# Weight slabs in a four-block transformer kernel: the low half written in place over the raw slab, slots refilled once their matmuls are done, high halves made three slabs ahead

## What is computed

```
def swiglu(h, w_gate, w_up, w_down):
    return (jax.nn.silu(h @ w_gate) * (h @ w_up)) @ w_down

def conformer_conv(h, w_pw1, b_pw1, w_dw, b_dw, ln_g, ln_b, w_pw2, b_pw2):
    u = h @ w_pw1 + b_pw1
    a, gate = jnp.split(u, 2, axis=-1)
    u = a * jax.nn.sigmoid(gate)
    u = lax.conv_general_dilated(
        u, w_dw[:, None, :].astype(u.dtype), window_strides=(1,),
        padding=((CONV_WIDTH - 1, 0),),
        dimension_numbers=("NWC", "WIO", "NWC"),
        feature_group_count=D_MODEL) + b_dw
    u = jax.nn.silu(layer_norm(u, ln_g, ln_b))
    return u @ w_pw2 + b_pw2
```

## Time and profile before

| | us |
|---|---|
| runs of the kernel before | 3374.32, 3394.07, 3396.99 |
| their median | 3394.07 |
| span of the profiled execution | 3392.2 |
| PE busy | 3157.2 |
| PE weight load busy | 2432.9 |
| DVE busy | 1679.6 |
| ACT busy | 1250.1 |
| POOL busy | 1270.3 |

### The profile page before, as it was taken

How to read it: one execution, slowest core, us unless ns; L and a number is a source line. 1 busy time by engine, 2 the same in 40 slices (tenths; PEclk the granted TensorE clock), 3 DMA queues, 4 the chain that set the end, 5 groups by cost and what they waited for, 6 DMA issues and landing times.

```text
span 3392.2 us, 41307 instructions
## 1 busy us (share of the span) xinstructions
PE 3157.2 (93%) x13970; PEld 2432.9 (72%) x13970; DVE 1679.6 (50%) x2266; ACT 1250.1 (37%) x1983; POOL 1270.3 (37%) x496
## 2 busy tenths in 40 slices
PE   7999999989898899999986899999989789899998
PEld 5656788866675578888754777888867468778886
DVE  6455555356517745443587635222353784352224
ACT  4344444223334424432322433443222443344422
POOL 3201444433431144434576423443433125144443
PEclk9998999999998999999998899999999899999999
DMA  3201222222220022223212311222322013122222
GB/s 138 90 11 35 89 93 93 83 84 74 90 72 1 9 91 93 89 87 90 75 49 69 104 64 66 95 93 82 93 87 78 32 45 111 44 93 92 93 80 75
DMA packets 73430, 257.30 MB, mean 76 GB/s; under 512 B 8544, under 2 KB 8808, under 8 KB 72944
## 3 DMA queue, kind: packets, MB, share of 16 engines
q1 hardware_dynamic: 68400, 244.87, 22.0%
q10 hardware_dynamic: 4928, 11.10, 0.9%
HBM read 253.82 MB, written 2.12 MB: 75 GB/s over the span
## 4 chain that ended last, share of the span: by engine, by line
PE 58%; issue 22%; DVE 9%; POOL 8%; ACT 2%; ACTq 1%; DVEq 0%; DMA 0%; POOLq 0%
PE bank L564 17%; PE bank L565 17%; PE bank L566 17%; POOL w_lo L499 7%; PE bank L613 1%; PE bank L640 1%; PE bank L774 1%; DVE xl L958 1%; DVE acc L965 1%; DVE a_stat L1021 1%; POOL m_lo L515 1%; ACT sq L1569 1%; PE bank L886 1%; DVE xt L991 1%; DVE a_prob_t L1046 0%
## 5 line engine op out<-in xcount | busy, mean ns | idle before, releaser
L499 POOL TENSOR_TENSOR w_lo<-w_raw,w_hi 128x1024 fp32r<-128x1024 f32 (+1 forms) x475 | 1212.0, 2560 | 1962.3 <-ACT w_hi L1578 1962.2
L564 PE MATMUL bank<-xh,w_hi 128*128 128x512 f32 x2328 | 949.3, 408 | 85.8 <-DVE xl L958 38.2
L565 PE MATMUL bank<-xl,w_hi 128*128 128x512 f32 x2328 | 930.4, 400 | 0.0
L566 PE MATMUL bank<-xh,w_lo 128*128 128x512 f32 x2328 | 929.9, 399 | 0.0
L1578 ACT ACTIVATE w_hi<-w_raw 128x1024 fp32r<-128x1024 f32 x475 | 493.8, 1054 | 1036.3 <-DVE xt L991 540.1
L564 PEld LDWEIGHTS bank<-xh,w_hi 128*128 128x128 f32 x2328 | 443.8, 191 | 218.8 <-issue 44.3
L565 PEld LDWEIGHTS bank<-xl,w_hi 128*128 128x128 f32 x2328 | 444.1, 191 | 111.9 <-issue 7.3
L566 PEld LDWEIGHTS bank<-xh,w_lo 128*128 128x128 f32 x2328 | 443.1, 190 | 108.6
L965 DVE TENSOR_TENSOR acc<-acc,sq 128x512 f32<-128x512 f32 x88 | 185.6, 2109 | 206.1 <-ACT sq L1569 206.1
L566 PE MATMUL bank<-hh,w_lo 128*128 128x512 f32 x704 | 279.1, 396 | 0.0
L564 PE MATMUL bank<-hh,w_hi 128*128 128x512 f32 x704 | 279.1, 396 | 0.0
(11 more groups left out here) (264 smaller groups left out, 4049.0 us busy)
## 6 DMA issues: line engine op xcount, KB each, us to landing
w_raw<-w_ffn_in SPq DMA_DIRECT2D x88, 512.0 KB, 3.4
w_raw<-w_glu_in SPq DMA_DIRECT2D x88, 512.0 KB, 3.4
w_raw<-w_ssm_in SPq DMA_DIRECT2D x41, 512.0 KB, 3.4
w_raw<-w_ffn_out SPq DMA_DIRECT2D x32, 512.0 KB, 3.6
w_raw<-w_mem_kv SPq DMA_DIRECT2D x32, 512.0 KB, 3.5
w_raw<-w_glu_out SPq DMA_DIRECT2D x32, 512.0 KB, 3.6
w_raw<-w_pw SPq DMA_DIRECT2D x24, 512.0 KB, 3.4
w_raw<-w_attn_in SPq DMA_DIRECT2D x18, 512.0 KB, 3.4
```

The lines of the kernel that those rows point to most:

```text
L499: pool.tensor_tensor(w_lo[:, slot, n], w_raw[:, slot, n], w_hi[:, slot, n].bitcast(F32), ALU.subtract).then_inc(w_split, 1)
L564: pe.matmul(b, wh, hi[:, k, 0:n], start=(k == 0), stop=False)
L565: pe.matmul(b, wh, lo[:, k, 0:n], start=False, stop=False)
L566: mm = pe.matmul(b, wl, hi[:, k, 0:n], start=False, stop=last)
```

## The change

`w_lo` now lies at the address of `w_raw`, so that POOL writes the low half over the raw slab it reads (`LEAD` = 3 is new). SP may therefore load slab s only once TensorE has used slab s-4, and waits for `w_used` in place of `w_split`. ACT makes halves three slabs ahead, not four: `next_half` in step c makes slab c+3 (with one slab per chunk). The wait for `w_used` of slab s-4 in `half` stays. In `residual`, `taps`, `gate`, `attn` and `ffn` the call of `next_half` moves ahead of the wait for the bank, and the second call in `ffn` ahead of the wait for `f_prod`. POOL's inserted work (`m_lo`, and the weights of the SSM stage) comes before the fourth slab of its stream, not the fifth. Weights with 22 blocks are padded with zeros to 24 on the host, so that every slab is loaded and split at full width; TensorE still multiplies 22. The 16 KB per partition that `w_lo` had are left free.

```diff
SLAB = 8
+LEAD = 3
...
         xt = sb("xt", [P, KD, S])
+        raw_at = cursor[0]
         w_raw = sb("w_raw", [P, SLOTS, SLAB * P])
         w_hi = sb("w_hi", [P, SLOTS, SLAB * P], F32R)
-        w_lo = sb("w_lo", [P, SLOTS, SLAB * P], F32R)
+        w_lo = nc.alloc_sbuf_tensor_at("w_lo", [P, SLOTS, SLAB * P], F32R, offset=raw_at)
...
                 def turn(i, chunks):
                     for j in range(chunks):
-                        k = 0
-                        for t, nb in enumerate(st.slabs):
+                        for t in range(st.per):
                             o = j * st.per + t
                             slot = (st.slab0 + o) % SLOTS
 
-                            sp.wait_ge(w_split, st.slab0 + o + 1 + i * 4 * st.per)
-                            src = w[ds(4 * i + j, 1), :, k * P:(k + nb) * P] if not isinstance(i, int) \
-                                else w[4 * i + j:4 * i + j + 1, :, k * P:(k + nb) * P]
-                            sp.dma_start(w_raw[:, slot, 0:nb * P], src.rearrange("a p n -> (a p) n")) \
+                            sp.wait_ge(w_used, st.slab0 + o + 1 + i * 4 * st.per)
+                            ks = slice(t * SLAB * P, (t + 1) * SLAB * P)
+                            src = w[ds(4 * i + j, 1), :, ks] if not isinstance(i, int) \
+                                else w[4 * i + j:4 * i + j + 1, :, ks]
+                            sp.dma_start(w_raw[:, slot, :], src.rearrange("a p n -> (a p) n")) \
                                 .then_inc(w_landed[slot], 16)
-                            k += nb
...
-                            if between is not None and o == SLOTS:
+                            if between is not None and o == LEAD:
                                 between()
                             s = st.slab0 + o
                             slot = s % SLOTS
-                            n = slice(0, nb * P)
-
                             pool.wait_ge(w_half, s + 1 + i * 4 * st.per)
-                            pool.tensor_tensor(w_lo[:, slot, n], w_raw[:, slot, n], w_hi[:, slot, n].bitcast(F32),
+                            pool.tensor_tensor(w_lo[:, slot, :], w_raw[:, slot, :], w_hi[:, slot, :].bitcast(F32),
                                                ALU.subtract).then_inc(w_split, 1)
...
             def next_half(st, j, i):
 
                 for t in range(st.per):
-                    o = st.slab0 + j * st.per + t + SLOTS
+                    o = st.slab0 + j * st.per + t + LEAD
...
                 def chunk(c, j, i):
 
+                    next_half(st, j, i)
                     act.wait_ge(bank_free, BANKS + st.chunk0 + c + 1)
-                    next_half(st, j, i)
                     body(c, j, i)
...
                 def taps(c, j, i):
-                    act.wait_ge(bank_free, BANKS + st.chunk0 + c + 1)
-
                     if not (isinstance(c, int) and 1 <= c < 3):
                         next_half(st, j, i)
+                    act.wait_ge(bank_free, BANKS + st.chunk0 + c + 1)
...
                 def gate(c, j, i):
+                    next_half(st, j, i)
                     act.wait_ge(bank_free, BANKS + st.chunk0 + c + 1)
-                    next_half(st, j, i)
...
                 def chunk(c, j, i):
                     if j >= 1:
                         fin(c - 1, j - 1)
+                    next_half(st, j, i)
                     act.wait_ge(bank_free, BANKS + st.chunk0 + c + 1)
                     if not (isinstance(c, int) and c >= 13):
                         if not isinstance(c, int) or c >= 2:
                             act.wait_ge(q_sum, c - 1)
                         act.activation(sq[:, j % 2, :], row(qk, c),
                                        ACT.Square).then_inc(q_sq, 1)
-                    next_half(st, j, i)
...
                         p = i * 2 + jj
+                        next_half(ST[si], 2 * jj, i)
                         act.wait_ge(bank_free, BANKS + ST[si].chunk0 + 2 * p + 1)
-                        next_half(ST[si], 2 * jj, i)
...
+                        next_half(ST[si], 2 * jj + 1, i)
                         act.wait_ge(f_prod, f0 + p + 1)
                         act.activation(row(hh, p), f_h[:], ACT.Copy)\
                             .then_inc(f_hi, 1)
-                        next_half(ST[si], 2 * jj + 1, i)
...
-            for t in range(1, min(SLOTS, SLABS)):
+            for t in range(1, min(LEAD, SLABS)):
                 half(t, t, 1)
...
     k, n = w.shape
+    if k % (SLAB * P):
+        w = np.concatenate([w, np.zeros((-k % (SLAB * P), n), w.dtype)], 0)
+        k = w.shape[0]
```

More of the change, by code:

```diff
@@ L504, in split_stream @@
                     turn(0, 4, first)
-                    if 4 * st.per <= SLOTS:
-                        first()
                 with pool.Fori(0 if first is None else 1, turns) as i:
```

## The result

| | before | after |
|---|---|---|
| median of the runs (20 each) | 3393.36 | 3415.41 |
| lowest to highest | 3374.32 to 3410.22 | 3402.69 to 3431.36 |
| span of the profiled execution | 3392.2 | 3418.1 |
| mean granted clock of TensorE | 0.967 | 0.961 |

The account below looks back on a forecast made before the run. TensorE was busy 3157 of 3392 us, with no steady stall to remove. Conf +47.5, boundaries -28, attn_in +5, ssm_in +2, memory streams +1 gave +27.5: span 3419.7, median 3421.6 us, range 3390 to 3450.

Parts of the forecast that it names:

- The loss in conf: Convolution stage: three ahead, each turn's fourth slab waits for POOL, kept out by VectorE's taps; +47.5 us.
- T+60.8: Conf: forecast start of the next turn, T being the first c_a of a turn; before it was 44.3.
- Rival 1: Conf: POOL gets in between the taps, the 47.5 us loss becomes about 0, total 3374 us; chance 0.14.
- The boundaries: Where streams meet: high halves made ahead of the bank wait leave the way to the new input; -28 us.
- rival 2: Boundaries: addition, acc and xl each come 2 us later beside POOL; gain 12 not 28, total 3437; chance 0.14.
- Square in attn_in: Three places in attn_in: a high half now precedes Square, +1.05 us each plus possible lower clock; +5 us.
- The SSM stage: ssm_in: tap chunks unchanged, TensorE one slab less ahead at the gates, the 1.81 us wait goes; +2 us.
- Loads behind the use, in place, padding: Slab loads waiting for matmuls, low half over the raw slab, full-width slabs: each taken as 0.
- Rival 3: Memory streams: slab refill sets the pace, some 26 chunks wait 0.8 us each; +20, total 3442; chance 0.10.
- +27.5: Whole kernel: sum of forecast terms, 47.5 - 28 + 5 + 2 + 1 us, on the span of 3392.2.

Follow-up runs that it names:

- e10: Kernel before, four ahead with its own low buffer, with every move of a high half ahead of the bank wait outside attn_in: 3362.44 us, 0.9889.
- e3: Kernel before, four ahead with its own low buffer, with only the `next_half` call in `residual` moved ahead of the bank wait: 3369.03 us, 0.9921.
- e8: Changed kernel with the four loads of rel rows issued at attn_in's chunk 3 instead of behind its last chunk: 3405.31 us, 1.0005.
- e11: Changed kernel with low halves in their own buffer and SP waiting for `w_split` again: 3420.47 us, 1.0044.
- e4: Kernel before with high halves three slabs ahead (`LEAD = 3`) and nothing else of the change: 3625.67 us, 1.0688.
- e2, e5, e7: Changed kernel with one of these, text not saying which: pauses between taps (3398.56 us); conf's fourth half before `c_diag` (3365.37); or a turn ahead, Square first (3360.59).
- e6: Changed kernel with Square back ahead of the high half in attn_in: 3411.06 us, 1.0044.
- e9: Changed kernel with conf's fourth half between sigmoids and tap matrices, Square first in attn_in, and rel loads at chunk 3: 3357.02 us, 0.9863.
- e12: Kernel before with the change's order outside attn_in and the rel loads at chunk 3 of attn_in: 3366.23 us, 0.9897.
- e1: Changed kernel with the fourth slab of each convolution turn made already in the turn before: 3378.39 us, 0.9926.

## Why the prediction was right, and where it was not

**The loss in conf: right.** T+60.8 was forecast for the turn, 61.5 measured; a wait of 16.2, measured 16.07 twice and 17.26 in the first turn; the sum +47.5, measured +49.8. The step on which all hung was that POOL gets nothing done while the taps run. The changed kernel shows it again (26.11, 25.94, 25.94 us), moving the half out of the way takes the loss out twice, and with pauses between the taps no low half takes over 2.925. Rival 1, POOL getting in between, is out for the taps as written.

The Trainium skill, page "SBUF — State Buffer", section "SBUF: two separate sides", has the two engines lock their shared ports for a whole instruction, whoever starts first. The trace agrees with the second half (2.41 us for the one that starts ahead of the taps), but for GpSimd as the loser the unit is the run of taps without a pause: 26.11 us, and 2.925 at most with 0.15 us pauses.

**The boundaries: right, a little small.** -28 forecast, -31.5 measured; the waits for xl at the entries of ssm_in, ffn_in1 and pw1 are gone, and `acc` at 1.75 beside the low half shows that rival 2 was wrong in its price: one us, not two for each of three instructions. What I did not see is that this part needs nothing else of the change.

**Square in attn_in: right.** Waits of 2.24 in three places (2.3 forecast), +3.9 with what goes with them (+5); with Square first again 5.2 us come back.

**The SSM stage: wrong in sign.** The step was "the tap chunks are paced by VectorE and ACT, whose order and work stay the same" and then up to a slab time of loss. The order does change: the high half no longer waits for VectorE's reading of the bank, and since TensorE in these chunks stands behind the low half, each chunk gets 0.2 us shorter and the gates lose their wait. That is -9.4 over the chunks by e10 against e3. Three ahead does cost what I had bounded by a slab time: slab 6's high half comes behind the first tap chunks (at 771.73; in e10, four ahead, at 745.24, in a stage that begins 3.9 us earlier), and TensorE waits 3.76 us for it; by the last chunk e10 and the changed kernel are 5.3 us apart. Net -3.5 in the chunks. Another -4.5 lies in the rest of the SSM stage behind them, the scan, of which e8 and e11, with the same chunks, have only -1.3. The rest is the clock: in the scan 34.1 us are at half clock in the changed kernel and 41.0 in e8 and e11 (and before). The scan of the changed kernel, then of e8, with as many matmuls:

```profile
985.58:1163.47 177.89, 147.80 (x738) 0.90 0.02 7
```

```profile
973.15:1154.28 181.13, 151.07 (x738) 0.89 0.02 7
```

So of the -8.0 about 3.2 us are a clock that no term of the prediction had, and 4.8 belong to the new order and the shorter lead together.

**Loads behind the use, in place, padding: 0 within what can be told.** With the first two taken back (the padding stays) the ratio is 1.0044 [1.0022, 1.0066] against 1.007 [1.0054, 1.0086]: 9 us, give or take 9, by these intervals, 8.2 by the spans, half of it in attention and its clock. Executions that had the same mean clock differ by less: at 0.963 four of e11 took 3411.05 to 3411.73 us, two of the changed kernel 3412.94 and 3413.24. Rival 3 did not come about: mem_kv0 is 1.1 us longer and mem_kv1 as long as before.

**The term that was missing: TensorE's clock in attention, +10.2 us** (with 1.3 for the longer wait ahead). The prediction priced the clock only behind pauses that it had itself found. Its sum of +27.5 comes so close to +25.9 by luck in part: this miss of +11.5 and that of the SSM stage, -10, cancel.

That the 10.2 us go with the clock can be read from all the traces together. The half-clock time of attention, and the length from the first rel matmul to the first matmul of attn_out: 27.3 us at half go with 146.9 to 147.0 (before, e3, e4, e8); 44.4 with 154.0 (e11); 51.2 with 156.8 to 157.2 (after, e2, e5, e7, e10); 71.7 with 160.6 to 162.9 (e6, e9, e12); 88.8 with 168.5 (e1).

**What stays open** is what sets that clock. It follows neither the load of a slab (e11 has none beside the first rel load, e10 has the one that e3 has) nor the stop ahead (1.93 us in e3 and 2.02 in e4 without half clock behind it, 1.90 in e11 and 1.98 in e10 with it, none in e8, e9 and e12). It is not fixed by the kernel either. Of the kernel before, run beside the experiments, 77 executions have their mean granted clock on record: from 0.973, at 3377.44 us, to 0.957, at 3419.90 us, and on the whole the time is the longer the lower the clock. Those of the changed kernel go from 0.968 (3402.69) to 0.955 (3431.36). So one kernel moves by far more than 10 us with its clock, and one trace of each cannot tell whether these 10 us belong to the change. Without them and without the 3.2 us of the scan the parts above add up to about +19 us, 8.6 under the forecast.

## What to carry to other kernels

When slabs are made fewer steps ahead, list for each stage which slab becomes the next needed one and what stands between its wait and its use in the program of the engine that makes it; one stage with a long block of other work (here 24 us of taps) can cost more than all others gain. Then ask whether the gain needs the change at all: here the order alone, one line in `residual`, gives 0.8% with four slabs ahead. The memory that the in-place buffer saves then costs no time that can be told, if the fourth half of a turn is moved out of the taps' way: 0.9863 [0.9827, 0.9898] with all three repairs, against 0.9889 [0.9846, 0.9932] for the order without the change, and these overlap. Where GpSimd is kept out beside VectorE, start its work first (here VectorE paid 2 us for it), or leave pauses; the pauses cost more here, and of the 50 us that were lost in conf only 37 came back, of which 18 went again in the stage behind it.

## What the runs showed of the hardware that I had not expected

- GpSimd's low half was kept out by VectorE's taps for as long as these followed without a pause, and let in at pauses of 0.15 us. It takes 2.4 us alone; it took 26.11 beside the taps, 2.925 at most with the pauses, and 2.41 when it started first. Then VectorE waited: 2.96 us for two taps in place of 1.00, and 2.60 to 2.90 for single taps in place of 0.75.
- The granted clock of attention changed between kernels whose work there is the same: 1.00 or 0.74 over 160 to 200 us, 0.81 or 0.50 over 240 to 312 us, with PE at least 92% busy in each. That moves the attention behind the rel wait by 7 to 22 us.
- The mean granted clock changed between executions of one kernel too, from 0.973 to 0.957, and the time with it from 3377.44 to 3419.90 us, 1.3%. A difference of 0.3% between two traces is therefore no evidence for or against an edit.
